# Two attention layers: projections and w_out as three fp32r passes over split weights, with the loads and steps reordered

## What is computed

```python
shift, scale, gate = jnp.split(c @ w_ada + b_ada, 3, axis=-1)
u = x * (1.0 + scale[:, None, :]) + shift[:, None, :]
h = split_cols(u @ w_in)
...
y = (mix * jax.nn.silu(h["gate"])) @ w_out
return layer_norm(ALPHA * x + (1.0 + gate[:, None, :]) * y, ln_g, ln_b)
```

## Time and profile before

| | us |
|---|---|
| three runs | 2137.88, 2145.98, 2149.16 (median 2145.98) |
| span of the profiled execution, first to last instruction | 2141.1 |
| the profiled execution's own time | not among the times shown |
| median above the span | 4.9 |
| TensorE busy / VectorE busy / ScalarE busy in the span | 2068.3 / 1508.6 / 1010.9 |
| layer 0 of attention with its start (0 to 284.8), layer 1 (284.8 to 531.2) | 284.8, 246.4 |

### The profile page before, as it was taken

The page is one execution under the profiler, slowest core; times in us unless marked ns, Lnnn a source line. Parts: engine busy times, 40 slices in busy tenths (PEclk is TensorE's granted clock), DMA queues, the critical chain, the costliest instruction groups (busy, mean ns, idle before and its releaser), DMA issues.

```text
span 2141.1 us, 26780 instructions
## 1 busy us (share of the span) xinstructions
PE 2068.3 (97%) x10468; PEld 1647.7 (77%) x10468; DVE 1508.6 (70%) x1833; ACT 1010.9 (47%) x1092; POOL 50.8 (2%) x56
## 2 busy tenths in 40 slices
PE   7999999999989999999988999999999999999996
PEld 4786577756876799888747888888888888888885
DVE  4565434554597545438858889888898889888887
ACT  1121312122223334313236777777777777777774
POOL 0000000000011000000200000000000000000000
PEclk9999999999999999999998999999999999999999
DMA  9844043611621365552138999999999999999991
GB/s 355 279 136 170 30 140 106 228 51 33 217 78 41 103 193 197 176 182 80 39 124 290 371 355 366 348 349 377 347 375 331 367 368 356 376 322 376 353 366 40
DMA packets 238750, 502.74 MB, mean 235 GB/s; under 512 B 11274, under 2 KB 53026, under 8 KB 238626
## 3 DMA queue, kind: packets, MB, share of 16 engines
q1 hardware_dynamic: 238626, 501.04, 65.6%
HBM read 499.96 MB, written 1.05 MB: 234 GB/s over the span
## 4 chain that ended last, share of the span: by engine, by line
PE 91%; DVE 7%; ACT 1%; issue 1%; DMA 0%; SPq 0%; DVEq 0%; ACTq 0%
PE bank L1549 14%; PE bank L1518 9%; PE bank L1520 9%; PE bank L1519 9%; PE bank L782 6%; PE bank L1221 6%; PE bank L1014 3%; PE bank L1089 3%; PE bank L790 3%; PE bank L1191 3%; PE bank L1197 3%; PE bank L1458 3%; PE bank L1429 2%; PE bank L1428 2%; PE bank L1427 2%; PE bank L1393 2%
## 5 line engine op out<-in xcount | busy, mean ns | idle before, releaser
L2766 DVE TENSOR_TENSOR ring_r<-ring,his 128x2048 fp32r<-128x2048 f32 x240 | 549.1, 2290 | 87.8 <-ACT his L1699 86.9
L1699 ACT ACTIVATE his<-ring 128x2048 fp32r<-128x2048 f32 x240 | 460.1, 1917 | 133.2 <-PE bank L1520 76.8
L1518 PE MATMUL bank<-his,xe_hi 128*128 128x512 f32 x896 | 353.7, 395 | 4.2 <-DVE ring_r L2766 4.2
L1520 PE MATMUL bank<-his,xe_lo 128*128 128x512 f32 x896 | 349.5, 390 | 0.0
L1519 PE MATMUL bank<-ring_r,xe_hi 128*128 128x512 f32 x704 | 274.2, 389 | 0.0
L2766 DVE TENSOR_TENSOR more_raw_r<-more_raw,his 128x2048 fp32r<-128x2048 f32 x96 | 220.0, 2291 | 28.7 <-ACT his L1699 28.2
L1699 ACT ACTIVATE his<-more_raw 128x2048 fp32r<-128x2048 f32 x96 | 184.1, 1918 | 54.8 <-PE bank L1549 29.3
L1518 PEld LDWEIGHTS bank<-his,xe_hi 128*128 128x128 f32 x896 | 168.3, 188 | 41.0 <-DVE ring_r L2766 5.4
L1520 PEld LDWEIGHTS bank<-his,xe_lo 128*128 128x128 f32 x896 | 168.2, 188 | 35.9
L1519 PEld LDWEIGHTS bank<-ring_r,xe_hi 128*128 128x128 f32 x704 | 132.2, 188 | 26.5
L1221 PE MATMUL bank<-uT,ring 128*128 128x256 f32 (+1 forms) x768 | 150.9, 359 | 0.0
(11 more groups left out here) (448 smaller groups left out, 3046.1 us busy)
## 6 DMA issues: line engine op xcount, KB each, us to landing
ring<-in_moe_w_gate_dram SPq DMA_DIRECT2D x96, 1024.0 KB, 5.4
...
ring<-in_w_in_dram SPq DMA_DIRECT2D x16, 2048.0 KB, 11.7
...
ring<-in_w_ada_dram SPq DMA_DIRECT2D x12, 2048.0 KB, 10.4
ring<-in_w_out_dram SPq DMA_DIRECT2D x8, 2048.0 KB, 9.7
```

The costliest lines, as they stand in the source:

```text
L1518: mm(bank[b][:, :], xe_hi[:, a, k, :], hi[:, kk, :], start=(k == 0), stop=False)
L1520: last = mm(bank[b][:, :], xe_lo[:, a, k, :], hi[:, kk, :], start=False, stop=(k == KD - 1))
L1699: return go(out, in_, ACT.Copy, scale=scale)
L2766: tt(piece_lo(s), piece_raw(s), piece_hi(s).bitcast(fp32), ALU.subtract).then_inc(S("lo_ready"), 1)
```

## The change

Every matmul of `w_in` and `w_out` in the two attention layers becomes three fp32r passes. `WEIGHT_PIECES` cuts each layer's weights into 42 pieces of up to 1024 elements per partition. ScalarE's `weights_hi` copies a piece into one of five places of `high` (w_out's into `out_hi`), and waits for the load of its weights and for the last use of the piece five before it. VectorE's `weights_lo` subtracts in place. Both walk the same fixed order of pieces, at points written into their lists. The tokens are split too (`uh`, `uT_r`), as is the input of w_out. The ring has four slots instead of five, and each load of the attention layers has its slot written out; the later blocks take the slots in the turn 0, 2, 3, 1. The fox values come first. The nsa values are made 402 columns wide (with the window keys in between, which are also made by `window_keys`), the gate's sums move into the group stage (`ADA_STEPS_AT`, `ADA_GATE_AT`), all eight gate parts lie in it, and layer 1's sums (`ada_sum`) move later in layer 0.

```diff
-W_IN_PARTS = [("idx_q", "idx_w"), ("dsa_q", "dsa_v"), ("fox_v", "fox_f"), ("fox_q", "fox_q"), ("fox_k", "fox_k"),
+W_IN_PARTS = [("fox_v", "fox_f"), ("idx_q", "idx_w"), ("dsa_q", "dsa_v"), ("fox_q", "fox_q"), ("fox_k", "fox_k"),
...
+SLOTS = 4
+HIGHS = 5
+HIGH = 1024
...
+PIECE_STEP = {"fv0": 1, "fv1": 2, "fv2": 3, "vs0": 4, "vs1": 5, "vs2": 6, "gate0.0": 7, "gate0.1": 7, "gate1.0": 8, "gate1.1": 8}
+NSTEP = 8
...
+GATE_PART_AT = {5: 0, 6: 1, 8: 2, 9: 3, 12: 4, 13: 5, 16: 6, 17: 7}
+GATE_COPY_AT = {8: 0, 11: 1, 15: 2}
+ADA_GATE_AT = {10: 0, 14: 1}
+ADA_STEPS_AT = {6: (4, 0, 4), 8: (4, 4, 8), 10: (5, 0, 4), 13: (5, 4, 8)}
+SELECT_AT = {n: (n + 1,) for n in range(5, 15)}
+SPLIT_HI_AT = {9: "gate1.2", 11: "gate1.3", 14: "wout0.1", 15: "wout0.3", 18: "wout1.1", 19: "wout1.3"}
...
+    add("fv0", 4); add("iq", 5); add("ff", 6); add("fv1", 7)
...
+    for q in range(4):
+        add_ada(0, q, q)
+    add_in(0, "fox_v", 0)
+    add_in(0, "idx_q", 1)
+    add_in(0, "dsa_q", 2)
+    add_in(0, "fox_q", 3)
+    add_ada(1, 0, 0)
+    add_in(0, "fox_k", 1)
+    add_ada(1, 1, 2)
+    add_in(0, "nsa_kc", 3)
+    add_ada(1, 2, 0)
+    add_in(0, "nsa_q", 1)
+    add_cmp(0, 2)
+    add_in(0, "nsa_vs", 3)
+    add_ada(1, 3, 0)
+    add_ada(0, 4, 1)
+    add_gate(0, 0, 2)
+    add_gate(0, 1, 3)
+    add_ada(0, 5, 0)
+    add_out(0, 0, 1)
...
+        def high_part(l, p):
+
+            part, k0, kn, _, width = WEIGHT_PIECES[p]
+            if p.startswith("wout"):
+                return out_hi[:, int(part[4:]), k0:k0 + kn, :]
+            at = ringed.index((l, p)) % HIGHS * HIGH
+            return high[:, at:at + kn * width].rearrange("p (k n) -> p k n", k=kn)
+
+        def low_part(l, p):
+
+            return part_of(ring_r, (l, p), WEIGHT_PIECES[p])
...
+            def feat(b, l, p, to, tokens=slice(0, T), a=0, n=P):
+
+                hi, lo = split(l, p)
+                o = b[0:n, to + tokens.start:to + tokens.stop]
                 for k in range(KD):
-                    last = mm(b[0:n, to + tokens.start:to + tokens.stop], w[:, k, a:a + n], uT[:, k, tokens],
-                              start=(k == 0), stop=(k == KD - 1))
+                    mm(o, hi[:, k, a:a + n], uh[:, k, tokens], start=(k == 0), stop=False)
+                    mm(o, hi[:, k, a:a + n], uT_r[:, k, tokens], start=False, stop=False)
+            def tok(o, l, p, i, a, n, first=True, final=True):
+
+                hi, lo = split(l, p)
+                _, k0, kn, _, _ = WEIGHT_PIECES[p]
+                own = slice(i * P, (i + 1) * P)
+                for kk in range(kn):
+                    k = k0 + kk
+                    mm(o, uh[:, k, own], hi[:, kk, a:a + n], start=(first and kk == 0), stop=False)
+                    mm(o, uh[:, k, own], lo[:, kk, a:a + n], start=False, stop=False)
+                    last = mm(o, uT_r[:, k, own], hi[:, kk, a:a + n], start=False, stop=(final and kk == kn - 1))
                 return last
...
+            def fox_values(l, i):
+
+                j = jobs[l, f"fv{i}"]
+                b = take(pe, j)
+                for k in range(KD // 2):
+                    if l == 0 and i == 0:
+                        pe.wait_ge(S("u_split"), k + 1)
+                    last = tok(b[:, 0:FOX_HEADS * HD], l, f"fv{k}", i, 0, FOX_HEADS * HD, k == 0, k == KD // 2 - 1)
+                    if i and k < KD // 2 - 1:
+                        last.then_inc(S("w_step"), 1)
+                done(last, j)
+
...
-                feats(l, "fq01", ("fox_q", 0, P), ("fox_q", P, P))
+                feats(l, "fq01", "fq0", "fq1")
+                rotate(l, "dq")
+                rotate(l, "dk")
...
+                feats(l, "fq2", "fq2")
                 if l == 0:
-                    shift_scale(1, 3)
+                    shift_scale(1, 0)
                 index_scores(2)
                 index_scores(3)
-                feats(l, "fk01", ("fox_k", 0, P), ("fox_k", P, P))
+                feats(l, "fk01", "fk0", "fk1")
                 index_scores(4)
                 index_scores(5)
-                feats(l, "fk2", ("fox_k", 2 * P, P))
+                feats(l, "fk2", "fk2")
                 index_scores(6)
                 index_scores(7)
+                if l == 0:
...
+            def weights_hi(l, upto):
+
+                while split_at[0] <= piece_order[l, upto]:
+                    ll, p = list(piece_order)[split_at[0]]
+                    part = WEIGHT_PIECES[p][0]
+                    n = load_at[ll, part]
+                    act.wait_ge(slot_loaded[slot_of[n]], loaded[ll, part])
+                    if p == "wout0.0":
+                        act.wait_ge(S("rope_done"), NR * (ll + 1))
+                        act.wait_ge(bank_full[jobs[ll, "S6"].bank], jobs[ll, "S6"].fill)
+                    elif p == "wout1.0":
+                        act.wait_ge(bank_full[jobs[ll, "S16"].bank], jobs[ll, "S16"].fill)
+                    elif not p.startswith("wout"):
+                        at = ringed.index((ll, p)) - HIGHS
+                        if at >= 0:
+                            lb, pb = ringed[at]
+                            if pb in PIECE_STEP:
+                                act.wait_ge(S("w_step"), NSTEP * lb + PIECE_STEP[pb])
+                            else:
+                                j = jobs[lb, PIECE_DONE[pb]]
+                                act.wait_ge(bank_full[j.bank], j.fill)
+                    copy(high_part(ll, p), raw_part(ll, p)).then_inc(S("w_hi"), 1)
+                    split_at[0] += 1
+
...
                     j = jobs[l, name]
                     free(copy(dst[:, tiles[0]:tiles[1], :], filled(act, j)[:, 0:(tiles[1] - tiles[0]) * T],
                               HD ** -0.5 if dst is fq else 1.0), j)
+                    weights_hi(l, ("kc", "vc", "nq0", "nq1")[n])
                     for r in (2 * n, 2 * n + 1):
                         j = jobs[l, f"is{r}"]
...
 
                 exps(0)
                 exps(1)
+                weights_hi(l, "vs0")
                 exps(2)
+                j = jobs[l, "ks"]
+                free(copy(raw["ks"][:, 0, :], filled(act, j)[:, 0:T]), j)
+                weights_hi(l, "vs1")
+                exps(3)
...
+            def weights_lo(l, upto):
+
+                while split_at[0] <= piece_order[l, upto]:
+                    ll, p = list(piece_order)[split_at[0]]
+                    dve.wait_ge(S("w_hi"), split_at[0] + 1)
+                    tt(low_part(ll, p), raw_part(ll, p), high_part(ll, p).bitcast(fp32), ALU.subtract).then_inc(S("w_lo"), 1)
+                    split_at[0] += 1
+
...
                 for n, (i, heads) in enumerate(ISCORES):
+                    if n in (2, 4, 6):
+                        weights_lo(l, {2: "vc", 4: "nq0", 6: "nq1"}[n])
                     if l == 0 and n == 2:
-                        shift_scale(1, 3)
+                        shift_scale(1, 0)
+                    if l == 0 and n == 4:
+                        ada_sum(1, 1)
...
+                weights_lo(l, "vs1")
+                if l == 0:
+                    ada_sum(1, 2)
                 row_max(3)
                 copy_pT(2)
                 mixed(1)
-                ada_steps(5, 2, 3)
+                weights_lo(l, "vs3")
+                if l == 0:
+                    shift_scale(1, 2)
                 row_max(4)
...
+                weights_lo(l, "gate0.2")
+                for step in range(4, 6):
                     select(step)
-
-                copied(dve, jobs[l, "kwg"])
...
-                    if n in SELECT_AT:
-                        select(SELECT_AT[n])
+                    for step in SELECT_AT.get(n, ()):
+                        select(step)
+                    if n in SPLIT_LO_AT:
+                        weights_lo(l, SPLIT_LO_AT[n])
+                    if n in ADA_STEPS_AT:
+                        q, a, z = ADA_STEPS_AT[n]
+                        for k in range(a, z):
+                            ada_step(l, q, k)
+                    if n - 1 in ADA_GATE_AT:
+                        dve.wait_ge(S("gate_bias"), 16 * (l + 1))
+                        gate(ADA_GATE_AT[n - 1])
...```

In layer 0's projections, ScalarE before, from the copy of the dsa keys to the second of the fox queries (`p_sb` holds the relu of the index scores, `fq` the fox queries):

```order
L1699 ACTIVATE raw_dk<-bank 64x256 [waits bank_full7]
L1699 ACTIVATE dv<-bank 128x128
...
L1699 ACTIVATE fq<-bank 128x512 [waits bank_full2]
L1779 ACTIVATE p_sb<-bank 128x256 [waits bank_full7]
L1779 ACTIVATE p_sb<-bank 128x256 [waits bank_full0]
L1699 ACTIVATE fq<-bank 128x256 [waits bank_full3]
```

551 lines of the change are left out of this document (336 added, 215 removed), and 3 rows, old and new, of the table PIECE_DONE.

## The result

| | before | changed |
|---|---|---|
| median of the runs, us | 2144.6 (2137.9 to 2149.2, 4 runs) | 2256.8 (2253.9 to 2257.9, 4 runs) |
| ratio, 95% interval | | 1.0521 [1.0498, 1.0543] |
| span of the profiled execution, us | 2141.1 | 2255.8 |
| mean granted TensorE clock | 0.978 | 0.931 |

A forecast was written before the change was run, and what follows sets the result against it. TensorE, busy for 2068.3 of 2141.1 us, was taken as the bound. Costs of 77 us (waits, groups, clock) against 57 saved gave +20 on 2145.98, so 2166 us, range 2122 to 2188.

The forecast's parts named there:

- What TensorE saves: Attention layers' projections, gates and w_out: cheaper fp32r passes save 29.5 us in layer 0 and 27.5 in layer 1, together -57.
- Clock: TensorE in attention: after four long waits matmuls run at 1.2 GHz, 1.3 us each, +5; bounds 0 and 15.
- The groups: Group stages: TensorE's and VectorE's lists both reach 69 us, groups take 79, +10 a layer; bounds 0 and 14.
- Two loads: Layer 0, `nsa_kc` and `nsa_q`: ScalarE's high halves wait for loads ahead of relus, 7.3 and 8.5 us, +16.
- The moved sums: Layer 0: `ada_sum` parts 1 to 3 delay what TensorE needs by 5.8, 5 and 12.5 us, +23; bounds 0 and 27.
- Start of the layers: Starts of layers 0 and 1 and w_out's input: TensorE waits for copies and splits of tokens, +3 and +4.
- nsa values and gate1: Ahead of the groups: late `nsa_vs` and gate1 loads make TensorE wait 3 us in each layer, +6.
- Layer 1 ten faster, layer 0 thirty slower: Attention layers: layer 1 shorter than 246.4 us by about 10, layer 0 longer than 284.8 by about 30.
- VectorE keeps up: Rival, 25%: VectorE's steps fit its idle gaps, the groups' 20 and sums' 23 us go; faster, 2123 us.
- The clock takes more: Rival, 12%: seven waits cost 2.4 us each and groups fall to the lower clock at times; +15 more, 2181 us.

The follow-up runs named there:

- open2: Changed kernel with gate copies earlier, VectorE's extra work before its copy of transposed weights, gate bias off bank 6, w_out's splits moved: 2211.9 us.
- fixes2: Changed kernel with reordered groups, relus first, sums of parts 1 to 3 on GpSimd, narrow passes widened, gate weights split behind `vblk`: 2164.5 us, 1.009 of before.

## Why the prediction was wrong

- *What TensorE saves, -57*: the prices held. At 2.4 GHz a pass starts every 0.120 us at 256 columns (forecast 0.120), 0.174 at 384 (0.174), 0.184 at 402 (0.181), 0.23 at 512 (0.227) and 0.112 at 8 (0.112); a feature unit is 24 x 0.120 = 2.9 us. At 1.2 GHz a pass takes 0.21 at 256 columns and at 8, and 0.43 at 512.
- *Clock, +5*: this is the step that failed most. It priced "each" of four waits at 1.3 us with bounds 0 and 15. TensorE's busy time should have fallen by 57 and rose by 24, so by the forecast's own prices 81 us more are spent at the lower level; the granted clock gives 84 by itself (96 after, 12 before). Both are estimates. The row it was priced from, a gate part of 6.06 instead of 3.63 us, is one gate part behind a thin stretch; where waits followed each other the granted clock was 0.71 and 0.75 over whole stages, and at the narrow passes it fell with no wait at all. The Trainium skill (TensorE: Matmul & The Clock Gate, What's actually happening) has the ramp at under 1% of a typical kernel's span; what the lower level adds here is by this estimate 3.6%, and the measurement decides.
- *The groups, +10 a layer*: they grew by 38.5 and 42.2. Lists laid "end to end group by group" took VectorE's lengths and left out that one bank passes between three engines. Taking the three copies out of that loop gave 19, more of the order 26 (open2), and VectorE was busy for 62%, not over 85%.
- *Two loads, +16*: shown where forecast, 15.7 us, each behind a ScalarE idle on a load of w_in for 10.3 and 9.3 us; but not additive: moving the relus ahead of them gave 4 to 6, and the rest came back ahead of `shift_scale`.
- *The moved sums, +23*: TensorE's idle ahead of `shift_scale` is 18.6 us, in waits of 4.2, 1.5 and 12.9 at the step's own places (forecast 5.8, 5 and 12.5). Removing the work gave 12, on GpSimd with its better start 21.
- *Start of the layers, +7, nsa values and gate1, +6*: waits of 1.8 and 3.6 us at the starts (forecast 3 and 4, with w_out's input) and of 9.3 on `vblk` in layer 1, where 3 were forecast. fixes2 shows the last for the place of the gate's halves in the two lists.
- *Layer 1 ten faster, layer 0 thirty slower*: from mix to mix layer 1 takes 279.7 us where it took 241.4, 38 longer; layer 0's mix comes 80 later.
- *The rivals*: "VectorE keeps up" failed, though VectorE was idle for 38% of the groups: the loop on bank 6 cost 19 us; shortened, VectorE's steps gave 15 us and its low halves 27. "The clock takes more" named the right cause at a quarter of its price: 5 and 15, since it took seven waits times 2.4, against 81.

Together: waits +92 (97 - 5), low clock about +81, work -57, which is the +116 of the stage sums; it closes by construction, since the 81 is what busy time rose above the forecast. The forecast had 72, 5 and 57: the waits were 20 us too small, the clock 76. That it was slower was forecast by waits of nearly the right sum, and at three places (both loads, the last `shift_scale`) to within 1 us; in the groups the wait was another one than forecast. How the 81 divide between waits and narrow passes is settled only for the four narrow places (14). Of the waits, what "held" the groups is settled only so far that neither VectorE's load nor bank 6 alone did.
